# Three banks for attention's logits, four rectified buffers, and the first modulations gathered group by group

## The chip, the cores and the metric

The kernel runs on one core of a Trainium2 chip. The metric is the device time of one execution in microseconds (us), the median of three runs. Engines are named as in the profile: PE is TensorE, DVE is VectorE, ACT is ScalarE, POOL is GpSimd, SP is SyncE, whose queue issues the transfers. PEld is PE's loading of weights.

## The reference

One inference step of a two-layer encoder, for 1024 prompt tokens and 64 sample tokens (the latter with 256 cached keys and a state). In each layer:

```python
shift, scale, gate = split(silu(c) @ w_ada + b_ada, 3)          # c: one vector for the prompt, one for the sample
h = rms_norm(x, g_pre) * (1 + scale) + shift
q_a, k_a, v_a, gate_a, q_i, k_i, w_i, q_b, k_b, v_b, gate_b = split_cols(h @ w_in)
# rope on q_a, k_a, q_i, k_i, q_b, k_b
score = sum_h relu(q_i[h] . k_i) * w_i[h] * IDX_SCALE           # the indexer, 4 heads
idx = top_k(score within the chunk-causal limit, min(256, S // 4))
o_a = softmax(q_a . k_a[idx] / 8) @ v_a[idx]                    # 8 heads of 64, 2 kv heads
o_b = group_norm(retention(q_b, k_b, v_b, state))               # 4 heads of 128, recurrent
y = rms_norm(concat(o_a * silu(gate_a), o_b * silu(gate_b)) @ w_out, g_post)
x = x + gate * y
```

The outputs are x after both layers, the new rotated keys, values and indexer keys, and the new states, for prompt and sample.

## The kernel before

**Tiles and steps.** x is cut into nine tiles of 128 tokens, eight of the prompt and one of the sample (tile 8). The columns of w_in and w_out are cut into ten chunks for each layer (`KIND`): one for the indexer (324 columns), four retention heads (512 each), the gate (512), two for attention (384) and two for the output (512). A step is one chunk for one tile, so there are 2 x 10 x 9 = 180 steps, chunk by chunk, and within a chunk tile by tile. Every engine's program is written out in the same loop `for i in range(-1, STEPS + 2)`, each step in four quarters `q`; work on step i+1's projection is interleaved with what follows steps i, i-1, i-2. Each engine works strictly in its own order; semaphores join them.

**Projection.** h and w are each split into a high and a low part (`h_hi`, `h_lo`, `w_hi`, `w_lo`), and `project` adds three products (two for the sample tile) into one of two PSUM banks `proj`. ACT makes the high part of a slice of weights (`split_weights`), POOL the low part (`lower_weights`); SP loads raw slices into three buffers (`load_raw`), each behind a wait for the slice three before.

**Before the first projection.** SP issues tables and vectors (`tables_landed`, 13 transfers), x tiles 0 and 1, and then 32 slices of w_ada (`ADA_FIRST`, in the order k outside, group inside) into nine slots of `ada_raw`, eight raw slices of w_in among them. PE transposes the vectors (bank `vec`), ACT makes silu(c), PE multiplies each slice (`ada`, L896) into one of four banks (`ada_banks`: both `proj`, both logit banks), one for each group of 512 columns: groups 0 and 1 are the shift, 2 and 3 the scale, for features 0 to 511 and 512 to 1023. When all is done ACT copies the four banks (L1308), PE turns them to columns (`ada_columns`, L902), DVE adds the bias (`modulate`, L1821) and makes the hidden tile (`take_hidden`, L1770, eight operations in two halves from the banks of `turn_hidden`, L910), ACT rounds it (`split_hidden`, L1138) and POOL makes the low part (`lower_hidden`, L1384). x tiles are squared on ACT (`square_x`, L1120, the squares themselves go to the bank `spare`, only their sum is used), the root is taken on POOL (L1394), and DVE norms x into one of two slots (`norm_input`, L1756). `spare` also takes the products of the later w_ada slices.

**Indexer steps.** DVE ropes the step's rows (`rope`, L1518 to L1535) first. For tiles 2 to 8 PE multiplies queries and keys, by head and by part of up to 512 keys (`dot_keys`, L950), two heads in a quarter, into the two `logit_banks`; ACT rectifies into one of two buffers `relu` (L1258); DVE multiplies by the head's weight and adds into `score` (`weigh_relus`, L1551 and L1554).

**The search.** In the retention and gate steps the 256th score of each query is searched bit by bit, for five tiles (one of them the sample tile) on DVE (`count_pass`, L1580) and for tiles 6 and 7 by sign tests on ACT (`test_bit`, L1287), bit n in the n-th retention step, settled on DVE (`settle_bit`).

**Attention steps.** PE's logits (L950) go to the same two banks; DVE adds the mask and takes the row maximum (`row_maxima`, L1724), which frees the bank; ACT takes the exponential (L1271), PE transposes it, ACT copies it (L1238), PE multiplies by the values (L975).

**Rings.** The banks for logits and for transposes are each a `Ring` of `RB = 2`. The keys of a ring are numbered in PE's order by `plan_units`; `wait_free` waits until the use two before has been taken. `dot_keys` asks for all banks of a quarter before its first matmul:

```python
for h, p in heads:
    logits.wait_free(pe, ("l", g, h, p))
for h, p in heads:
    ...
```

and ACT's rectifying waits for the buffer two before:

```python
if n >= 2:
    act.wait_ge(relu_used, n - 1)
```

## Time and profile before

| | us |
|---|---|
| median of three runs | 1540.69 |
| lowest, highest | 1540.31, 1542.75 |
| the profiled execution | 1545.81 |
| its span, first to last instruction | 1544.0 |
| PE busy in it | 1409.0 |
| DVE busy | 1045.1 |
| ACT busy | 786.5 |
| POOL busy | 411.1 |

The mean granted clock of PE in the profiled execution was 0.981 of full speed. The engines' busy times overlap; a stage's length is set by whichever of them, or whichever chain through several, ends last in it. In windows, the columns are the stretch and its length, then the busy time (and instructions) of PE, PEld, DVE, ACT and POOL, the granted clock, the DMA engines' share and GB/s. In a timeline, square brackets hold the idle time of the engine before the row and what ended it.

### The profile page before, as it was taken

Reading aid. Unit: us, or ns where it says so; the run is one execution under the profiler, and the core shown is the slowest. Engines: PE = TensorE matmul, PEld = TensorE weight load, DVE = VectorE, ACT = ScalarE, POOL = GpSimd, SP = SyncE. Lnnn points to the kernel's source line nnn. Section 1 sums busy time; section 2 is a strip of 40 time slices with the busy share of each in tenths; the row PEclk is TensorE's granted clock in tenths of the full one; section 3 lists DMA queues with packets and bytes.
Section 4 is the critical chain, followed back from the end, with each engine's and each line's share of the span. In section 5 each row is a group of like instructions: output and inputs, shape, how many; then the busy total and the mean of one; then the engine's idle time right before and its main releaser. Section 6 shows DMA issues by size and latency. Waiting matters only on the chain.

```text
span 1544.0 us, 24320 instructions
## 1 busy us (share of the span) xinstructions
PE 1409.0 (91%) x7591; PEld 1063.4 (69%) x7591; DVE 1045.1 (68%) x3018; ACT 786.5 (51%) x1916; POOL 411.1 (27%) x360
## 2 busy tenths in 40 slices
PE   6778999999999889889996899999999988988995
PEld 1654777777887567557875567878888756755884
DVE  0687899999996446542287789999998644654224
ACT  2445666666226456554453566666622655555421
POOL 2441233433421001001188114444442101100100
PEclk9899999999999999999998999999999999999998
DMA  9321343423232112112252111211122211211324
GB/s 325 98 69 30 111 130 101 125 89 104 54 86 60 39 31 67 54 56 96 83 184 68 32 44 34 63 45 36 55 66 79 59 32 34 67 59 56 110 69 163
DMA packets 125191, 122.04 MB, mean 79 GB/s; under 512 B 33257, under 2 KB 94025, under 8 KB 125065
## 3 DMA queue, kind: packets, MB, share of 16 engines
q1 hardware_dynamic: 125064, 120.49, 25.8%
q8 instruction: 63, 1.03, 0.3%
q14 instruction: 64, 0.52, 0.1%
HBM read 93.55 MB, written 26.90 MB: 78 GB/s over the span
## 4 chain that ended last, share of the span: by engine, by line
PE 53%; DVE 31%; issue 5%; ACT 5%; DMA 4%; SPq 1%; DVEq 0%; POOL 0%; ACTq 0%
PE proj L931 10%; PE proj L932 10%; PE proj L934 9%; PE turn L910 8%; PE logit L950 6%; DVE U L1580 5%; PE out_bank L975 4%; DVE U L1770 2%; DVE by_cos_sin L1518 2%; DVE by_cos_sin L1520 2%; DVE turned L1535 2%; DVE score L1554 2%; DVE probsT_more L1653 1%; DMA U<-x_dram 1%; ACT probsT_more L1238 1%
## 5 line engine op out<-in xcount | busy, mean ns | idle before, releaser
L931 PE MATMUL proj<-w_hi,h_hi 128*128 128x512 f32 (+2 forms) x1440 | 578.7, 402 | 2.7 <-ACT U L1174 1.4
L932 PE MATMUL proj<-w_lo,h_hi 128*128 128x512 f32 (+2 forms) x1440 | 538.4, 374 | 0.0
L934 PE MATMUL proj<-w_hi,h_lo 128*128 128x512 f32 (+2 forms) x1280 | 480.2, 375 | 0.0
L1378 POOL TENSOR_TENSOR w_lo<-w_raw,w_hi 128x512 fp32r<-128x512 f32 (+2 forms) x160 | 207.5, 1298 | 832.4 <-ACT w_hi L1130 832.3
L931 PEld LDWEIGHTS proj<-w_hi,h_hi 128*128 128x128 f32 x1440 | 274.2, 190 | 62.1 <-issue 23.3
L932 PEld LDWEIGHTS proj<-w_lo,h_hi 128*128 128x128 f32 x1440 | 274.8, 191 | 31.0
L934 PEld LDWEIGHTS proj<-w_hi,h_lo 128*128 128x128 f32 x1280 | 242.8, 190 | 37.0
L1580 DVE TENSOR_SCALAR_CACHE_REDUCE U<-score,cand 128x384 bf16<-128x384 f32 x310 | 222.6, 752 | 2.2
L950 PE MATMUL logit<-keys,queries 64*128 64x512 f32 (+4 forms) x592 | 141.9, 555 | 42.5 <-DVE row_max L1724 22.8
L1238 ACT ACTIVATE probsT_more<-turn 128x512 f32<-128x512 f32 (+3 forms) x156 | 73.4, 491 | 160.2 <-PE turn L910 128.0
L910 PE MATMUL turn<-ident,U 128*128 128x128 f32 x672 | 107.5, 288 | 17.6 <-ACT probsT_more L1238 8.0
L910 PEld LDWEIGHTS turn<-ident,U 128*128 128x128 f32 x672 | 78.9, 146 | 63.5 <-issue 49.8
L1518 DVE TENSOR_TENSOR by_cos_sin<-rows,cos_b 128x256 f32<-128x256 f32 (+1 forms) x126 | 66.0, 524 | 78.3 <-ACT rows L1178 75.2
L1394 POOL TENSOR_TENSOR rstd<-means,minus_half 128x3 f32<-128x3 f32 (+2 forms) x53 | 40.8, 770 | 264.4 <-DVE means L1706 147.2
L950 PEld LDWEIGHTS logit<-keys,queries 64*128 64x128 f32 x592 | 46.8, 189 | 83.0 <-issue 32.7
L1130 ACT ACTIVATE w_hi<-w_raw 128x512 fp32r<-128x512 f32 (+2 forms) x160 | 95.1, 595 | 14.3 <-DMA w_raw<-in_w_in_dram 14.3
L910 PE MATMUL turn<-ident,turned 128*128 128x128 f32 x306 | 57.7, 286 | 37.1 <-DVE turned L1535 29.5
L1724 DVE CUSTOM_DVE_ANT_0 U<-logit,score 128x512 f32<-128x512 f32 (+3 forms) x108 | 61.8, 582 | 34.4 <-PE logit L950 34.2
L1271 ACT ACTIVATE U<-U,neg_max 128x384 f32<-128x384 f32 (+7 forms) x108 | 81.5, 754 | 3.1 <-DVE neg_max L1729 3.1
L910 PEld LDWEIGHTS turn<-ident,turned 128*128 128x128 f32 x306 | 37.3, 143 | 66.4 <-DVE turned L1535 38.3
L1287 ACT ACTIVATE U<-score,cand 128x896 bf16<-128x896 f32 x62 | 64.5, 1040 | 33.8 <-DVE cand L1618 33.7
L975 PE MATMUL out_bank<-probsT_more,U 128*64 128x256 f32 x468 | 75.2, 385 | 0.0
(173 smaller groups left out, 2055.0 us busy)
## 6 DMA issues: line engine op xcount, KB each, us to landing
w_raw<-in_w_in_dram SPq DMA_DIRECT2D x80, 256.0 KB, 3.2
probsT_more<-in_w_ada_dram SPq DMA_DIRECT2D x64, 256.0 KB, 3.9
score<-mixed_dram SPq DMA_DIRECT2D x36, 256.0 KB, 3.0
score<-in_w_ada_dram SPq DMA_DIRECT2D x32, 256.0 KB, 5.3
w_raw<-in_w_out_dram SPq DMA_DIRECT2D x32, 256.0 KB, 3.3
U<-in_x_prompt_dram SPq DMA_DIRECT2D x14, 512.0 KB, 4.0
mixed_dram<-U SPq DMA_DIRECT2D x24, 192.0 KB, 2.1
gates_dram<-U SPq DMA_DIRECT2D x18, 256.0 KB, 2.2
```

The lines of the kernel that those rows point to most:

```text
L910: ins = nc.tensor.transpose(turns.bank(key)[:, n * P:(n + 1) * P], piece, ident[:])
L931: nc.tensor.matmul(out, h_hi[:, k, tile], hi, start=(k == 0), stop=False)
L932: ins = nc.tensor.matmul(out, h_hi[:, k, tile], lo, start=False, stop=(t == SAMPLE and k == KT - 1))
L934: ins = nc.tensor.matmul(out, h_lo[:, k, tile], hi, start=False, stop=(k == KT - 1))
L950: logits.filled(nc.tensor.matmul(logits.bank(key)[:, 0:m], queries[rows_, HILO[g] % 2, h // 2, :], keys[rows_, k0 + a:k0 + a + m], start=T ...
L975: ins = nc.tensor.matmul(out_bank[HD * pair:HD * pair + HD, 0:256], v, probsT[part + pair][:, :, b * P:(b + 1) * P], start=(kb == 0), stop ...
L1130: nc.scalar.activation(w_hi[:, s % WS, 0:w], w_raw[:, n % RAWS, 0:w], ACT.Copy).then_inc(w_hi_ready, 1)
L1238: turns.take(nc.scalar.activation(probsT[2 * (u % 2) + h // 2][:, h % 2, 0:m], turns.bank(key)[:, 0:m], ACT.Copy), key)
L1271: nc.scalar.activation(probs[n % 4][:, 0:w], probs[n % 4][:, 0:w], ACT.Exp, bias=neg_max[:, n % 4:n % 4 + 1], scale=ATT_SCALE, accum_out=r ...
L1378: nc.gpsimd.tensor_tensor(w_lo[:, s % WS, 0:w], w_raw[:, n % RAWS, 0:w], w_hi[:, s % WS, 0:w].bitcast(F32), ALU.subtract).then_inc(w_lo_re ...
L1518: do(nc.vector.tensor_tensor(by_cos[:, 0:w].rearrange("p (h n) -> p h n", n=half), src.rearrange("p (h n) -> p h n", n=half), cs, ALU.mult))
L1580: ins = nc.vector.tensor_scalar(found[:, n % 2, 0:valid_keys(t)], s, cand[:, j:j + 1].bitcast(F32) if b else 0.0, extra(t), ALU.is_ge, ALU ...
```

## The change

1. **Logit rings.** Attention's logits get a ring of their own over three banks: the two logit banks and `spare`. The indexer's and the retention's stay in a ring of two over the same two banks. `Ring` takes its length from its banks. Where one ring's use follows the other's, PE waits until the last units of the other have been taken.
2. **Squares.** Since `spare` is now attention's, the squares in output steps and those of x for layer 1 are written to SBUF, as bf16, into the first slot of `rows`.
3. **Rectified buffers.** `relu` has four buffers instead of two. They reach into space that the sign tests and `ada_row` use, so their first user waits until all rectified logits have been weighed.
4. **Search.** The sign test of bit n on ACT moves from the n-th retention step to the one after it.
5. **The beginning.** The identity, the columns and the eight small vectors are issued on ACT's queue; SP's first transfer is a slice of w_ada. The slices come group by group, in the order 0, 2, 1, 3; x0 is issued behind slice 7, x1 behind slice 15, raw slices of w_in from slice 9 on; the rotary tables and the causal mask come after the last slice. Each group is copied on ACT when its eight slices are done and turned to columns among the slices of the next groups. The first half of tile 0 (features 0 to 511) needs groups 0 and 2 only; DVE, ACT and POOL make it before groups 1 and 3 are complete. Tile 1's transposes on PE move into the first step's second quarter.

```diff
-ADA_FIRST = [(0, grp, k) for k in range(KT) for grp in range(4)]
+FIRST_GROUPS = (0, 2, 1, 3)
+ADA_FIRST = [(0, grp, k) for grp in FIRST_GROUPS for k in range(KT)]
...
+ATT_LOGITS = [key for key in LOGITS if key[0] == "l" and kind(key[1]) == "att"]
+LOGITS = [key for key in LOGITS if key not in set(ATT_LOGITS)]
...
+RELUS = 4
...
-    n = (lct(g)[1] - RET0) * NT + lct(g)[2]
-    return n if n < BITS else None
+    n = (lct(g)[1] - RET0) * NT + lct(g)[2] - 1
+    return n if 0 <= n < BITS else None
...
+    def place(self, key):
+        return self.at[key] % len(self.banks), self.at[key] // len(self.banks)
...
-        relu = U[:, 4096:5120].rearrange("p (s n) -> p s n", s=2)
+        square_dump = rows[:, 0, :].bitcast(BF16)[:, 0:512]
+        relu = [U[:, 4096:4608], U[:, 4608:5120], U[:, 5120:5632], probs_last[:, 0:512]]
...
+        att_logits = Ring([*logit_banks, spare], ATT_LOGIT_AT, att_full, att_taken)
...
         @block.sync
         def _(sp):
-            for dst, src in ((cos_b, t_cos_b), (sin_b, t_sin_b),
-                             (ident, t_ident), (causal, t_causal), (cols, t_cols)):
-                sp.dma_start(dst[:], src).then_inc(tables_landed, 16)
...
-            load_input(0)
-            load_input(1)
...
                 sp.dma_start(ada_raw[:, a % ADAS, :], w_ada[l, k * P:(k + 1) * P, grp * 512:(grp + 1) * 512])\
                   .then_inc(ada_landed[a % ADAS], 16)
-                if a >= 5 and a % 2 and raw < KT:
+                if a in (7, 15):
+                    load_input(a // 8)
+                if a >= 9 and a % 2 and raw < KT:
                     load_raw(raw)
                     raw += 1
+            for dst, src in ((cos_b, t_cos_b), (sin_b, t_sin_b), (causal, t_causal)):
+                sp.dma_start(dst[:], src).then_inc(tables_landed, 16)
...
+                if heads[0] == (0, 0) and lct(g)[1:] == (ATT0, 0):
+                    for key in [k for k in LOGITS if k[1] < g][-RB:]:
+                        logits.wait_taken(pe, key)
+                    pe.wait_ge(ada_copied, len(ADA_GROUPS))
+                if heads[0] == (0, 0) and lct(g)[1:] == (0, SEARCHED[0]) and lct(g)[0]:
+                    for key in [k for k in ATT_LOGITS if k[1] < g][-3:]:
+                        att_logits.wait_taken(pe, key)
...
-            for a, (l, grp, k) in enumerate(ADA_FIRST):
-                pe.wait_ge(ada_landed[a % ADAS], 16 * (a // ADAS + 1))
-                ada(ada_banks[grp], grp, k, ada_raw[:, a % ADAS, :])
-            for grp in range(4):
-                pe.wait_ge(ada_rows_ready, grp + 1)
-                ins = ada_columns(out_bank[:, 8 * grp:8 * grp + 8], ada_rows[grp])
-            ins.then_inc(ada_used, 1)
...
-            turn_hidden(0, 0)
-            turn_hidden(0, 1)
+            def turn_group(n):
+                grp = FIRST_GROUPS[n]
+                pe.wait_ge(ada_rows_ready, n + 1)
+                ada_columns(out_bank[:, 8 * grp:8 * grp + 8], ada_rows[grp]).then_inc(ada_turned, 1)
+
+            for a, (l, grp, k) in enumerate(ADA_FIRST):
+                pe.wait_ge(ada_landed[a % ADAS], 16 * (a // ADAS + 1))
+                ada(ada_banks[grp], grp, k, ada_raw[:, a % ADAS, :])
+                if a % KT == 3 and a > KT:
+                    turn_group(a // KT - 1)
+                if a == 3 * KT - 1:
+                    turn_hidden(0, 0)
+            turn_group(3)
+            pe.wait_ge(ada_turned, 4)
...
+                    if i == -1 and q == 1:
+                        turn_hidden(0, 1)
...
         @block.scalar
         def _(act):
+            for dst, src in ((ident, t_ident), (cols, t_cols)):
+                act.dma_start(dst[:], src).then_inc(rows_landed, 16)
...
-                nc.scalar.activation(spare[:], src, ACT.Square, scale=D ** -0.5, accum_out=total).then_inc(signal, 1)
+                nc.scalar.activation(dump, src, ACT.Square, scale=D ** -0.5, accum_out=total).then_inc(signal, 1)
...
-                        if n >= 2:
-                            act.wait_ge(relu_used, n - 1)
+                        if n >= RELUS:
+                            act.wait_ge(relu_used, n - RELUS + 1)
...
-            for t in (0, 1):
-                wait_x(act, t)
-                square_x(t)
-            for s in range(KT):
-                split_weights(s)
-            for grp in range(4):
-                act.wait_ge(ada_used, len(ADA_FIRST) - 4 + grp + 1)
-                nc.scalar.activation(ada_rows[grp], ada_banks[grp][:], ACT.Copy).then_inc(ada_rows_ready, 1)
+            copy_group(0)
+            wait_x(act, 0)
+            square_x(0)
+            for s in range(4):
                 split_weights(s)
+            copy_group(1)
+            wait_x(act, 1)
+            square_x(1)
+            for s in range(4, KT):
+                split_weights(s)
+            split_half(0)
+            copy_group(2)
+            copy_group(3)
+            split_half(1)
             for t in (2, 3):
                 wait_x(act, t)
                 square_x(t)
-            split_hidden(0, 0)
...
+            modulate_half(0)
+            take_hidden(0, 0, (0,))
+            modulate_half(1)
+            take_hidden(0, 0, (1,))
             norm_input(2, mean_squares(2 + XLAG, 1, 2))
             take_hidden(0, 1)
+            dve.wait_ge(tables_landed, 16 * 3)
```

`copy_group(n)` copies group `FIRST_GROUPS[n]` once its eight slices are multiplied, `split_half(u)` is one half of the former `split_hidden(0, 0)`, and `modulate_half(u)` adds the bias and the pre-gain for half the features, behind the columns of two groups.

## Rows read from the trace of the kernel before

**Rows 1.** The page, busy time and share of each engine

```profile
PE 1409.0 (91%) x7591; PEld 1063.4 (69%) x7591; DVE 1045.1 (68%) x3018; ACT 786.5 (51%) x1916; POOL 411.1 (27%) x360
```

**Rows 2.** Windows by stage: indexer, retention, attention of layer 0; indexer of layer 1

```profile
47.70:149.40 101.70, 77.21 (x402) 55.86 (x403) 76.50 (x167) 48.10 (x115) 40.52 (x32) 0.92 0.24 67
149.40:408.20 258.80, 257.07 (x1371) 200.43 (x1370) 233.81 (x792) 154.35 (x356) 92.52 (x87) 1.00 0.34 101
456.50:688.50 232.00, 209.72 (x1274) 146.04 (x1273) 125.02 (x396) 125.14 (x341) 23.56 (x17) 0.98 0.18 50
812.00:898.50 86.50, 67.41 (x354) 48.17 (x355) 65.56 (x136) 39.91 (x97) 38.06 (x27) 0.94 0.21 51
```

**Rows 3.** Windows of the beginning; last three columns PEclk, DMA share, GB/s

```profile
2.00:4.00 2.00, 0.00 (x0) 0.00 (x0) 0.00 (x0) 0.39 (x1) 0.00 (x0) 1.00 1.03 358
5.00:6.00 1.00, 0.00 (x0) 0.00 (x0) 0.00 (x0) 0.00 (x0) 0.00 (x0) 1.00 0.09 22
12.80:20.00 7.20, 7.11 (x18) 1.46 (x18) 0.75 (x1) 0.95 (x2) 1.96 (x3) 1.00 1.05 378
32.00:38.80 6.80, 6.80 (x22) 1.28 (x19) 0.00 (x0) 1.79 (x3) 0.00 (x0) 1.00 1.05 398
```

**Rows 4.** Timeline of the beginning: start, us, engine, line, operation

```profile
0.72 0.39 SPq L684 DMA_DIRECT2D cos_b<-in_t_dram  x1
...
6.71 2.87 SPq L747 DMA_DIRECT2D score<-in_w_ada_dram  x6
...
6.89 0.42 PE L1033 MATMUL turn<-ident,U 96*128 96x96 f32 x1 [6.89 <-DMA U<-in_g_post_dram]
...
12.79 2.04 PE L896 MATMUL proj<-score,probs_last 128*32 128x512 f32 x3 [5.48 <-DMA score<-in_w_ada_dram]
...
38.87 0.60 ACT L1308 ACTIVATE probs_last<-logit 128x512 f32<-128x512 f32 x1
...
41.46 1.03 PE L902 MATMUL out_bank<-cols,probs_last 128*128 128x2 f32 x8
...
43.10 2.64 DVE L1770 TENSOR_SCALAR U<-turn,pre_scale,pre_shift 128x128 f32<-128x128 f32 x8
...
49.00 0.75 DVE L1756 TENSOR_SCALAR U<-U,rstd 128x1024 f32<-128x1024 f32 x1 [3.19 <-POOL h_lo L1384]
```

**Rows 5.** Timeline, later slices of w_ada on PE

```profile
152.21 1.06 PE L896 MATMUL spare<-probsT_more,probs_last 128*32 128x512 f32 x8
```

**Rows 6.** Groups by line, 92 to 150 us; last: idle before, what ended it

```profile
L1554 DVE SCALAR_TENSOR_TENSOR score<-U,w_idx,score 128x512 f32<-128x512 f32 (+3 forms) x27 | 19.6, 724 | 12.0 <-ACT U L1258 10.0
```

**Rows 7.** The same, 845 to 899 us

```profile
L1554 DVE SCALAR_TENSOR_TENSOR score<-U,w_idx,score 128x512 f32<-128x512 f32 (+3 forms) x30 | 19.7, 658 | 9.9 <-ACT U L1258 7.1 <-DVE score L1554 0.5
```

**Rows 8.** Windows of the last two indexer steps of layer 0

```profile
129.12:139.21 10.09, 9.01 (x43) 4.96 (x42) 7.06 (x16) 5.66 (x14) 0.00 (x0) 1.00 0.13 31
139.21:150.00 10.79, 9.67 (x41) 5.22 (x41) 7.53 (x13) 5.78 (x14) 1.47 (x1) 1.00 0.20 51
```

**Rows 9.** Waits of PE: in total, times, longest

```profile
PE logit L950 <- DVE row_max L1724: 22.8, 16, 2.9
```

**Rows 10.** Timeline of an attention step

```profile
548.42 0.68 DVE L1724 CUSTOM_DVE_ANT_0 U<-logit,score 128x512 f32<-128x512 f32 x1
...
549.03 0.68 DVE L1724 CUSTOM_DVE_ANT_0 U<-logit,score 128x512 f32<-128x512 f32 x1
...
549.87 2.08 PE L950 MATMUL logit<-keys,queries 64*128 64x512 f32 x4 [2.94 <-DVE row_max L1724]
```

**Rows 11.** Groups by line: a square into PSUM, a copy into SBUF

```profile
L1120 ACT ACTIVATE spare<-proj 128x512 f32<-128x512 f32 x36 | 21.4, 594 | 0.0
...
L1189 ACT ACTIVATE score<-proj 128x512 f32<-128x512 f32 x18 | 10.7, 595 | 42.4 <-PE proj L934 40.9 <-DVE proj L1790 1.5
```

**Rows 12.** Timeline of ACT in the first retention step of layer 0

```profile
150.42 0.97 ACT L1287 ACTIVATE U<-score 128x896 bf16<-128x896 f32 x1
...
152.39 0.78 ACT L1258 ACTIVATE U<-logit 128x320 f32<-128x320 f32 x2
```

More of the change, by code:

```diff
@@ L373, in __init__ @@
         self.banks, self.at, self.full, self.taken = banks, at, full, taken
+    def place(self, key):
+        return self.at[key] % len(self.banks), self.at[key] // len(self.banks)
     def bank(self, key):
[L376 removed]
+        return self.banks[self.place(key)[0]]
     def wait_free(self, eng, key):
[L379 to L381 removed]
+        slot, turn = self.place(key)
+        if turn:
+            eng.wait_ge(self.taken[slot], turn)
     def wait_full(self, eng, key):
[L384 to L385 removed]
+        slot, turn = self.place(key)
+        eng.wait_ge(self.full[slot], turn + 1)
     def wait_taken(self, eng, key):
[L388 to L389 removed]
+        slot, turn = self.place(key)
+        eng.wait_ge(self.taken[slot], turn + 1)
     def filled(self, ins, key):
[L392 removed]
+        ins.then_inc(self.full[self.place(key)[0]], 1)
     def take(self, ins, key):
[L395 removed]
+        ins.then_inc(self.taken[self.place(key)[0]], 1)
 class Stores:
@@ L572, in build @@
         logit_taken = [sem(f"logit_taken{n}") for n in range(RB)]
+        att_full = [sem(f"att_full{n}") for n in range(3)]
+        att_taken = [sem(f"att_taken{n}") for n in range(3)]
         relu_used = sem("relu_used")
@@ L949, in dot_keys @@
                     key = ("l", g, h, p)
-                    logits.filled(nc.tensor.matmul(logits.bank(key)[:, 0:m], queries[rows_, HILO[g] % 2, h // 2, :],
+                    ring.filled(nc.tensor.matmul(ring.bank(key)[:, 0:m], queries[rows_, HILO[g] % 2, h // 2, :],
                                                    keys[rows_, k0 + a:k0 + a + m], start=True, stop=True), key)
@@ L1189, in take_projection @@
                     nc.scalar.activation(dst, src[:], ACT.Copy)
-                    square(src[:], squares[:, t, 0, half:half + 1], proj_taken, g + 1)
+                    square(src[:], squares[:, t, 0, half:half + 1], proj_taken, g + 1, square_dump)
             def square_x(n):
@@ L1195, in square_x @@
                 for u in (0, 1):
-                    square(xt(n)[:, u * 512:(u + 1) * 512], squares[:, t + XLAG, 1, u:u + 1], x_squared, 2 * n + u + 1)
+                    square(xt(n)[:, u * 512:(u + 1) * 512], squares[:, t + XLAG, 1, u:u + 1], x_squared, 2 * n + u + 1,
+                           spare[:] if n < NT else square_dump)
             def take_turn(g):
@@ L1255, in middle @@
                         logits.wait_full(act, key)
-                        if n >= 2:
-                            act.wait_ge(relu_used, n - 1)
-                        logits.take(nc.scalar.activation(relu[:, n % 2, 0:m], logits.bank(key)[:, 0:m], ACT.Relu), key)
+                        if n >= RELUS:
+                            act.wait_ge(relu_used, n - RELUS + 1)
+                        logits.take(nc.scalar.activation(relu[n % RELUS][:, 0:m], logits.bank(key)[:, 0:m], ACT.Relu), key)
                         relu_count[0] += 1
@@ L1475, in take @@
                 ring.take(ins, key)
-                n = ring.at[key]
-                last[0] = (ring.taken[n % RB], n // RB + 1)
+                slot, turn = ring.place(key)
+                last[0] = (ring.taken[slot], turn + 1)
             def fence():
```

117 lines of the change are left out of this document (68 added, 49 removed).

## The prediction

> **What bounds the kernel now.** I read the page's busy shares first [rows 1]: TensorE (PE) is busy for 91% of the span, VectorE (DVE) for 68%, and no other engine for more than 51%. Busy shares are means over stages, so the second view is the windows, one for each stage [rows 2]. The reader is to compare PE's busy time with the length of each stretch. In layer 0's retention steps PE is busy 257.07 of 258.80 us: nothing but less PE work helps there, and the change takes no PE work away. In its indexer steps PE is busy 77.21 of 101.70 us at a mean granted clock of 0.92, DVE 76.50; layer 1's are much alike, 67.41 and 65.56 of 86.50. In the attention steps PE is busy 209.72 of 232.00. So waits can be taken out in three places: before the first projection, in the indexer steps, in the attention steps. Whatever they save is kept, since the stages follow each other in every engine's order and nothing waits for a clock time.
>
> The third view is the timeline and the windows of the first 50 us [rows 3, 4]; the fourth the groups by line in the indexer steps [rows 6, 7]; the fifth PE's own waits [rows 9]; and last one attention step in the timeline [rows 10].
>
> **The beginning.** SP issues 13 small tables and vectors from 0.72 us on and two rows of x, and the first slice of w_ada only at 6.71 [rows 4]. The DMA engines were full from 2 to 4 us (share 1.03, the 0.8 MB of rotary tables) and almost idle at 5 to 6 us (0.09); from 12.8 on they run at 1.05 and 378 GB/s, at the end at 398 [rows 3]. That PE is not the limit shows in a later row: eight such matmul instructions, four slices, take 1.06 us when their data are there [rows 5], 0.27 us for a slice, while 256 KB at 388 GB/s take 0.68. So this stretch is the DMA stream, and its tail is serial: the last group's copy starts on ScalarE (ACT) at 38.87, its columns on PE end at 42.49, DVE makes the hidden tile from 43.10 to 45.74, and only when GpSimd (POOL) has lowered it (xn has two slots) DVE norms tile 2, at 49.00 after 3.19 us of waiting [rows 4]. From there DVE has hardly a pause until the retention steps.
>
> After the change SP's first issue is a slice of w_ada. The stream has to bring 32 slices of 256 KB (8.39 MB), x0 and x1 (1.05), eight raw slices of 162 KB (1.33) and 0.15 of vectors and identity: 10.9 MB, or 28.1 us at 388 GB/s (the mean of the two windows). Full from about 2.2 us (as in [rows 3], 2 to 4 us), it ends at 30.3. The three tables (0.83 MB) come behind it; the first rope is their first reader, and now it is behind several more microseconds of work.
>
> What can make the stream run dry: SP may issue nine slices and x0, 2.9 MB, which last until about 9.7 us; then it waits for PE to free a slot. PE needs the vectors, now issued on ACT's queue: ten issues of some 0.4 us from 0.7 on (an issue of a table costs 0.39 [rows 4]), last one at about 4.3. Before they were all landed at 6.89. I take the same 7 us, so PE starts on slices at 7.8 and releases nine at 0.27 us each. SP then issues behind the wait; its raw slices 3 to 7 wait for POOL to lower slice n-3, and on ACT those splits now stand behind the copies of groups 0 and 1 and the squares of x0 and x1. Each such hold-up is 1 to 2 us, and mostly covered by up to nine slices in flight. I add 1.2 us for it: the last slice is used at 31.5, 7.3 us earlier than now.
>
> The tail: copy of the last group 0.7, its columns 1.03, the small modulation ops 0.61 (42.49 to 43.10), then half a tile, four of the eight ops of 2.64 us, 1.32: DVE is through at 35.2 against 45.74 now [rows 4]. The other half was made in the stream's shade: its groups 0 and 2 come first, and split and lowering run on ACT and POOL, which have no other work there. Next, ACT splits the second half (0.6) and squares x2 (two passes of 0.6 us [rows 11] and the reading of each sum, 1.6), the root costs about 1 us on DVE and POOL, and the norm of tile 2 starts at 38.4 against 49.00. **Term: 10.6 us.** Lower bound: if the stream's holes cost 5 us instead of 1.2, 6.8. Upper: 12, if there is none and PE's earlier projection of tile 0 also spares DVE its pause before tile 2.
>
> At this place a rule of the Trainium skill speaks against part of it. "DMA: Bandwidth & Descriptors", section "Issuing engines are not separate DMA queues", says that the queues share 16 engines and that issuing from several saves only sequencer time, usually small beside the transfer. The trace agrees with the first half (share 1.05, nothing to gain in rate) and contradicts the "usually small" here: engines idle at share 0.09 while SP issues. By the rule, with issue time worth nothing, the beginning would gain what rival 2 gains.
>
> **Four rectified buffers.** Now ACT may write rectified logits only two ahead of DVE. At the start of an indexer step DVE does the rope first, so the buffers stay full, ACT stands, the two banks stay full, PE stands, and when DVE comes to weigh heads 2 and 3 they are not there. DVE waited for a rectified logit 10.0 us in layer 0's steps and 7.1 in layer 1's [rows 6, 7]. With four buffers both pairs of a step are rectified before DVE starts to weigh; PE then fills the banks for the next pair while DVE weighs, and DVE should hardly wait. Bounds: 17.1 us if DVE is the limit everywhere. It isn't in the last indexer step of each layer: PE is busy 9.67 of 10.79 us there, because the first projection of the next stage is already 512 wide, against 9.01 of 10.09 (partly stretched by waits) one step before [rows 8]. That caps it. I take off 2 us for each layer: **term 13 us**, range 7 (the step becomes PE-bound through the logits' banks, of which there remain two) to 17.
>
> **Three banks for attention's logits.** PE waited 22.8 us for a row maximum, 16 times [rows 9]. In the row shown, two maxima start at 548.42 and 549.03 (the second ends at 549.72), and PE's pair of heads, which asks for both banks, starts at 549.87 [rows 10]. With a third bank in the ring the second matmul of a pair needs only the first maximum of the pair before: 0.61 us earlier, the distance of the two. The rest of the wait stays, because the rope still stands ahead of the first maximum on DVE. Sixteen waits with a mean of 1.43 us and a longest of 2.9: 16 x 0.61 = 9.8 if each is long enough; some aren't, I count 13. **Term 7.9 us**; from 4, if what follows (the transposed probabilities' copy on ACT) ends last in half of these steps, to 11, if the lower granted clock behind the long waits disappears (the four instructions at 549.87 take 2.08 us).
>
> **Squares into SBUF.** 54 of ACT's squares no longer go to the spare bank. The row of a square from PSUM into PSUM has 594 ns, a copy of equal width from PSUM into SBUF 595 [rows 11]: 54 x 1 ns, nothing. The Trainium skill, "ScalarE: Activation LUTs", section "Step-by-step: what each stage is for", says that ACT writes PSUM with lower latency than SBUF; it gives no figure. The measured rows show no such difference, and the waits sit in ACT's slack.
>
> **The later search.** The two sign tests of a bit leave the first retention step, where they stand ahead of the sample tile's rectified logits on ACT (tests from 150.42, rectifying from 152.39 [rows 12]), and come to a step that had none. That is 2.0 us on ACT in each layer; this stretch is nearly PE-bound, so I take 0.5 each, **1 us**, bounds 0 and 4. The step that gets the tests has cover for them in ACT's slack; with none it would be 0.
>
> **New waits on PE** at the first attention and the first searched indexer step ask for banks released steps before; nothing. Tile 1's transposes move behind the first two quarters of the projection; they need what DVE has done by then.
>
> **Sum.** 10.6 + 13 + 7.9 + 1 = 32.5 us. The profiled execution took 1545.81 us (span 1544.0), so 1513.3 in its terms; it stands 5.1 above the median of 1540.69, which gives **1508.2 us**.
>
> **Rivals.**
> 1. *Partly absorbed.* The indexer steps turn PE-bound after half the gain (6.5) and the attention steps hand back half (4): 10.6 + 6.5 + 4 = 21 us, 1519.6. For it: PE's 9.67 of 10.79. Against: one step before, PE has slack, and PE's own waits are what inflates its busy time.
> 2. *The stream gains only bytes and tail.* PE starts late, because vectors queue behind big slices, or raw slices hold SP: then only the three tables' bytes (0.83 MB, 2.1 us) and the shorter tail (10.6 - 7.3 = 3.3) are gained, 5.4 instead of 10.6: 27 us in all, 1513.4. It decides if PE's first slice is later than about 9.7 us.
> 3. *More than forecast.* The lower clock in the indexer and attention steps (means 0.92 and 0.98 [rows 2]) goes away with the long waits: another 8 us, 1500.
> 4. *Slower.* The clock goes the other way: many short PE gaps in place of a few long ones, and the granted clock stays at the lower level (1.2 GHz) in attention. A PE-bound microsecond at that level does half a microsecond's work, so to eat 32.5 us it needs 65 us more of it than now, and 100 us of it in the two attention stages would give +17 us, 1558. Against: the change shortens PE's waits and adds none, and the retention steps show 1.00.
> 5. *Nothing.* The ring of three is filled in pairs and relu's are not ahead because ACT stands elsewhere, and the stream restarts slowly: within 3 us. It needs all of these, hence little.
>
> **Numbers.** Forecast 1508.2: 0.50. Rival 1: 0.20. Rival 2: 0.13. Rival 3: 0.11. Rival 4: 0.03. Rival 5 with what I have missed: 0.03. The terms' own bounds give 18 to 44 us off; the range that leaves out no more than two in ten is 1498 to 1525. A measurement of this kernel tells a change of 0.2%, 3 us, from none. Faster 0.94, the same 0.03, slower 0.03.
>
> **What would show it.** Right: first slice matmul at about 8 us and the last copy of a modulation group at about 32; the norm of tile 2 at 38; DVE's idle time ahead of the weighing ops near 3 us instead of 17; PE's wait for row maxima at 15 us instead of 22.8, in as many places; the retention stages unchanged in length. Wrong: a gap in the DMA share between 8 and 30 us; PE's idle time in the indexer steps now before the transposes or before ACT's copies; an attention step of equal length with another releaser; a granted clock under 0.9 in a stage that had 1.00. The likeliest single error is the indexer term, where I could not see how much of PE's busy time is work.

## The result, and the profile after

The changed kernel took 1517.14 us in the median of four runs (1513.14 to 1518.44), the kernel before 1540.58 (1540.31 to 1542.75). The ratio is 0.984 with a 95% interval of 0.982 to 0.9861: faster, by 23.4 us between the medians. The forecast was 1508.2, with a range of 1498 to 1525. Timed twice more on other occasions, the changed kernel had 0.9848 (0.9827 to 0.9869) and 0.9825 (0.9807 to 0.9843).

The profiled execution took 1513.14 us (span 1511.3), 32.7 less than the profiled execution before. That this is all but the predicted 32.5 is luck: it is the fastest of its four runs, and the one before stood 5.1 above its median. The times of the runs decide, the traces say in which stage.

The page, busy times [rows 1]:

```profile
PE 1398.7 (93%) x7591; PEld 1058.8 (70%) x7591; DVE 1046.3 (69%) x3021; ACT 784.6 (52%) x1916; POOL 410.7 (27%) x360
```

Windows of the stages of [rows 2] (indexer, retention and attention of layer 0, indexer of layer 1), with the boundaries moved to where the stages now lie:

```profile
42.00:137.70 95.70, 75.57 (x395) 54.83 (x394) 77.04 (x168) 50.56 (x125) 41.17 (x33) 0.93 0.24 72
137.70:396.40 258.70, 256.97 (x1370) 200.31 (x1369) 233.38 (x792) 154.54 (x355) 92.78 (x87) 1.00 0.33 101
444.60:669.70 225.10, 206.89 (x1274) 143.96 (x1273) 124.97 (x396) 125.20 (x341) 23.54 (x17) 0.99 0.18 52
790.00:876.00 86.00, 70.15 (x377) 49.93 (x376) 68.91 (x142) 42.20 (x101) 40.19 (x28) 0.94 0.20 51
```

The retention stretch of layer 0 has kept its length, 258.70 against 258.80 us, and PE fills it as before. PE executes the same 7591 instructions, and is busy 206.89 us in attention where it was 209.72. What went is idle time and, in attention, time at the lower clock (the means of the three other windows are 0.93, 0.99 and 0.94 against 0.92, 0.98 and 0.94).

Stage lengths are read more sharply from ACT's copies of the projection, which come once in a step. The first copy of the indexer and of the retention, layer 0, in the kernel before and then after:

```profile
53.40 0.42 ACT L1160 ACTIVATE rows<-proj 128x324 f32<-128x324 f32 x1
...
149.53 0.51 ACT L1168 ACTIVATE rows<-proj 128x384 f32<-128x384 f32 x1
```

```profile
48.68 0.42 ACT L1196 ACTIVATE rows<-proj 128x324 f32<-128x324 f32 x1
...
137.67 0.51 ACT L1204 ACTIVATE rows<-proj 128x384 f32<-128x384 f32 x1
```

96.13 us in the one, 88.99 in the other. The table has such differences of the first copies of two stages, in us, of this profile and of those of the experiments below:

| from copy to copy | before | after | after_again | begin_only | rest_only | relu2 | att2 |
|---|---|---|---|---|---|---|---|
| start of the first | 53.40 | 48.68 | 49.72 | 48.98 | 52.95 | 49.47 | 48.53 |
| indexer, layer 0 | 96.13 | 88.99 | 90.66 | 98.12 | 87.72 | 97.79 | 89.80 |
| attention, layer 0 | 232.02 | 225.11 | 224.87 | 232.48 | 225.39 | 224.86 | 232.41 |
| indexer, layer 1 | 86.35 | 81.73 | 82.84 | 86.46 | 82.20 | 87.51 | 81.76 |
| attention, layer 1 | 230.53 | 224.85 | 224.83 | 230.87 | 225.10 | 225.07 | 229.63 |
| output, layer 1 | 114.29 | 113.87 | 113.85 | 114.28 | 113.87 | 113.87 | 113.89 |

So in this profile the beginning gave 4.7 us by the first copy, the indexer steps 7.1 and 4.6, the attention steps 6.9 and 5.7. The forecast had 10.6, 13 and 7.9.

The beginning in the timeline, rows that answer to [rows 4]:

```profile
4.34 0.32 ACTq L1136 DMA_DIRECT2D U<-in_g_post_dram  x1
...
5.04 6.77 SPq L749 DMA_DIRECT2D score<-in_w_ada_dram  x2
...
8.71 0.42 PE L1047 MATMUL turn<-ident,U 96*128 96x96 f32 x1 [8.71 <-DMA U<-in_g_post_dram]
...
9.55 3.64 PE L902 MATMUL proj<-score,probs_last 128*32 128x512 f32 x16 [0.41 <-ACT vec L1145]
...
37.82 0.60 ACT L1343 ACTIVATE probs_last<-logit 128x512 f32<-128x512 f32 x1 [3.31 <-PE logit L902]
...
44.28 0.75 DVE L1814 TENSOR_SCALAR U<-U,rstd 128x1024 f32<-128x1024 f32 x1 [0.66 <-POOL rstd L1451]
```

Windows of it, as in [rows 3], and SP's waits in the first 34 us (in total, times, longest):

```profile
10.00:11.00 1.00, 1.00 (x8) 0.20 (x4) 0.00 (x0) 0.00 (x0) 0.00 (x0) 1.00 0.39 150
11.00:12.00 1.00, 1.00 (x8) 0.20 (x4) 0.00 (x0) 0.00 (x0) 0.00 (x0) 1.00 0.01 2
12.00:13.00 1.00, 1.00 (x9) 0.20 (x2) 0.00 (x0) 0.00 (x0) 0.00 (x0) 1.00 0.47 129
13.00:19.00 6.00, 4.99 (x18) 1.26 (x13) 1.51 (x2) 2.76 (x7) 1.42 (x3) 1.00 0.92 281
```

```profile
SPq L749 <- PE proj L902: 7.5, 5, 6.0
SPq L721 <- POOL w_lo L1435: 5.0, 5, 2.1
```

To be seen: the last vector is issued at 4.34 us and PE is released by the vectors at 8.71, not at 7. By then SP has issued nine slices and x0 and stands 6.0 us in its tenth. The DMA engines then run dry: they have a share of 0.39, 0.01 and 0.47 in the three microseconds after 10, and 281 GB/s until 19. The last group's copy starts at 37.82, 1.05 us before that of the kernel before [rows 4]. Behind it everything went as worked out: the norm of tile 2 is 6.5 us behind the copy (predicted 6.9), where it was 10.1.

The waits for rectified logits in layer 0's and layer 1's indexer steps, groups by line, to be read against [rows 6] and [rows 7], and PE's waits for row maxima against [rows 9]:

```profile
L1612 DVE SCALAR_TENSOR_TENSOR score<-U,w_idx,score 128x512 f32<-128x512 f32 (+3 forms) x20 | 17.2, 863 | 4.4 <-ACT U L1295 3.1
```

```profile
L1612 DVE SCALAR_TENSOR_TENSOR score<-U,w_idx,score 128x512 f32<-128x512 f32 (+3 forms) x20 | 13.9, 698 | 4.4 <-ACT U L1295 3.1
```

```profile
PE logit L964 <- DVE row_max L1782: 9.4, 8, 2.3
...
PE spare L964 <- DVE row_max L1782: 5.0, 4, 2.3
```

DVE waited 3.1 us in each layer instead of 10.0 and 7.1 (4.7 in layer 0 in after_again). PE waited 9.4 + 5.0 = 14.4 us for row maxima instead of 22.8, in 12 places instead of 16.

### The profile page after: what moved, and what is told of

The parts are those of the page before. It is cut to its first block, busy times and chain, and to the rows that moved or that the text cites. A ratio compares the mean times of both kernels' runs of the same rounds, so it can differ in the third digit from the quotient of the medians.

```text
span 1511.3 us, 24328 instructions
## 1 busy us (share of the span) xinstructions
PE 1398.7 (93%) x7591; PEld 1058.8 (70%) x7591; DVE 1046.3 (69%) x3021; ACT 784.6 (52%) x1916; POOL 410.7 (27%) x360
## 4 chain that ended last, share of the span: by engine, by line
PE 56%; DVE 28%; issue 5%; ACT 5%; DMA 4%; POOL 0%; SPq 0%; DVEq 0%; ACTq 0%; POOLq 0%
PE proj L937 11%; PE proj L938 11%; PE proj L940 10%; PE turn L916 8%; DVE U L1638 5%; PE logit L964 5%; PE out_bank L989 5%; DVE U L1828 2%; DVE by_cos_sin L1576 2%; PE spare L964 2%; DVE by_cos_sin L1578 2%; DMA U<-x_dram 1%; DVE turned L1593 1%; DVE probsT_more L1711 1%; ACT probsT_more L1275 1%
## 5 line engine op out<-in xcount | busy, mean ns | idle before, releaser
L1325 ACT ACTIVATE probsT_more<-score,cand 128x1024 bf16<-128x1024 f32 x62 | 70.4, 1135 | 0.0
```

Source lines behind the costliest of these rows:

```text
L1325: nc.scalar.activation(tested[n % 2][:, 0:valid_keys(t)], scores(t)[:, 0:valid_keys(t)], ACT.Sign, bias=cand[:, col:col + 1].bitcast(F32) ...
```

## The experiments

There were eleven runs, of nine kernels (the changed kernel and rest_only ran twice), in three groups; each group was timed beside the kernel before on the same chip (medians 1542.91, 1541.97 and 1543.66 us). A ratio below is to these; 0.001 of it is 1.5 us. A label stands for a run and for its kernel.

**1 and 2. The change cut in two.** begin_only is the kernel before with part 5 of the change alone, rest_only the changed kernel without it:

```diff
 # begin_only
+FIRST_GROUPS = (0, 2, 1, 3)
+ADA_FIRST = [(0, grp, k) for grp in FIRST_GROUPS for k in range(KT)]
...
 # rest_only
-FIRST_GROUPS = (0, 2, 1, 3)
-ADA_FIRST = [(0, grp, k) for grp in FIRST_GROUPS for k in range(KT)]
+ADA_FIRST = [(0, grp, k) for k in range(KT) for grp in range(4)]
```

(with all that belongs to the beginning: the queues, copy_group, turn_group, the halves of tile 0).

> The kernel before with the change's beginning alone (issues on ACT's queue, slices group by group, half a tile early). Theory from the two traces: the stream ran dry from 10 to 13 us, so the beginning brings 4.7 us, 1535.9 against 1540.6. The forecast's term was 10.6: 1530.0; if the other parts of the change disturb the beginning, it should show here.

> Everything but the beginning. Theory: what the changed kernel has left, 23.4 - 4.7 = 18.7 us, so 1521.9. Rival: the parts are not additive, since another beginning moves where the lower granted clock falls in later stages; then begin_only and rest_only together bring more or less than 23.4 by 3 us or more.

begin_only: 1540.72 us, ratio 0.9986 (0.9974 to 0.9998), 2.2 us. rest_only: 1518.14, 0.9843 (0.982 to 0.9865), 24.2 us. The beginning fell far short of 10.6, and of the 4.7 that the first two profiles had let expect; its interval is 0.3 to 4.0 us. The rest brought a little more than its 21.9, and 5 us more than the 18.7 expected of it. Together they are 26.4 us, where the three timings of the changed kernel gave 24.6, 23.4 and 27.0: whether the two halves add up can't be told from these. In begin_only's timeline PE is released by the vectors at 9.93:

```profile
9.93 0.42 PE L1024 MATMUL turn<-ident,U 96*128 96x96 f32 x1 [9.93 <-DMA U<-in_g_post_dram]
```

By the first copy begin_only is 4.4 us ahead of the kernel before, but its indexer steps then take 98.12 us instead of 96.13: they had a granted clock of 0.50 in the first step and 0.82 from 100 us on, where the kernel before had 0.88 and 0.89:

```profile
49.00:59.10 10.10, 7.72 (x28) 7.27 (x29) 6.86 (x12) 3.85 (x11) 7.97 (x7) 0.50 0.27 76
...
100.00:147.00 47.00, 39.39 (x163) 23.87 (x164) 32.07 (x63) 20.14 (x50) 6.80 (x6) 0.82 0.11 26
```

```profile
53.40:63.60 10.20, 5.90 (x33) 5.35 (x31) 7.49 (x15) 3.98 (x11) 8.08 (x7) 0.88 0.26 76
...
103.00:149.50 46.50, 36.67 (x163) 21.63 (x164) 32.83 (x64) 20.88 (x51) 7.47 (x7) 0.89 0.11 26
```

**3 and 4. One ring shortened at a time.** The changed kernel with two rectified buffers, and with two banks for attention:

```diff
 # relu2
-RELUS = 4
+RELUS = 2
 # att2
-        att_logits = Ring([*logit_banks, spare], ATT_LOGIT_AT, att_full, att_taken)
+        att_logits = Ring(logit_banks, ATT_LOGIT_AT, att_full, att_taken)
...
-                    for key in [k for k in ATT_LOGITS if k[1] < g][-3:]:
+                    for key in [k for k in ATT_LOGITS if k[1] < g][-2:]:
```

> The changed kernel with two rectified buffers instead of four. Theory: the indexer steps and the first retention step lose again what the traces gave them (7.1 + 4.6 us, 11.7), 1528.8. Rival: PE's bound and the two remaining logit banks give half of it in any case, 1523. The attention stages must not change in length.

> The changed kernel with attention's ring cut to the two logit banks. Theory: 8.4 us of PE's waits for row maxima come back, 1525.5, with 22 to 23 us of waits as before. Rival: the trace's 12.6 us of shorter attention stages are all the third bank's, clock included, and 1529.7 comes out. The indexer steps must not change.

relu2: 1528.01 us, 0.9908 (0.9885 to 0.9932). att2: 1527.87, 0.9908 (0.9886 to 0.993). Against the changed kernel's three ratios (0.984, 0.9848, 0.9825) each part is worth 0.0060 to 0.0083, 9 to 13 us; the expectations were 11.7 for the buffers and 8.4 or 12.6 for the bank. The stage table puts them in their places: without the four buffers the indexer steps take 97.79 and 87.51 us, 11.8 more in sum than in after_again and 14.6 more than in the first profile; without the third bank attention takes 232.41 and 229.63, 12.3 more than in after_again. Each undoing leaves the other's stages alone. The groups of relu2 in layer 0's indexer steps and the waits of att2 show the mechanisms come back whole:

```profile
L1612 DVE SCALAR_TENSOR_TENSOR score<-U,w_idx,score 128x512 f32<-128x512 f32 (+3 forms) x30 | 23.0, 767 | 14.0 <-ACT U L1295 11.6
```

```profile
PE logit L964 <- DVE row_max L1782: 22.8, 16, 2.9
```

11.6 us of waiting for rectified logits again, and the same 22.8 in 16 places as [rows 9].

**5 to 7. The vectors' queue.** The changed kernel again; the six vectors of bias and gains issued on SP ahead of the slices (identity, columns and the two conditions stay on ACT); and all ten small transfers on SP:

```diff
 # split_vectors (sp_vectors: the identity, the columns and the conditions as well)
         def _(sp):
+            r = 2 * KT
+            for l in range(DEPTH):
+                for src in (b_ada, g_pre, g_post):
+                    n = src.shape[1] // P
+                    sp.dma_start(vec_rows[r:r + n, :], ...).then_inc(rows_landed, 16)
+                    r += n
...
         def _(act):
-            for l in range(DEPTH):
-                for src in (b_ada, g_pre, g_post):
-                    n = src.shape[1] // P
-                    act.dma_start(vec_rows[r:r + n, :], ...).then_inc(rows_landed, 16)
-                    r += n
```

> The changed kernel once more, beside the same runs of the kernel before as the next three. Before's runs spread over 9 us (1538.7 to 1547.7), so a single profiled execution of either may stand some 5 us off its median. Expected 1517 to 1520; a span 3 us or more above the first profile's 1511.3 would come from the steps of the indexer stage, where a GpSimd operation that starts just before VectorE's ropes may cost 2 us (1.22 and 1.56 us instead of 0.23 and 0.48).

> The changed kernel with six of the small vectors issued on SP ahead of the slices, four transfers left on ACT's queue. Theory: the vectors landed late (8.7 us, 4.3 after their last issue) because they were issued behind slices on full engines; so PE freed no slot until 11 us and the engines stood idle from 10 to 13 us. Then here the vectors land by about 5, the stream starts 2 us later but never stops, and the last copy of a group comes 3 us earlier, 34.8 instead of 37.8: 1514.5. Rival: the stream's rate, not the hole, is the limit (229 to 313 GB/s after it, with raw slices among them), and it ends at 37 to 38 as before.

> All ten small transfers on SP ahead of the slices, none on ACT's queue; otherwise the changed kernel. Theory: the first slice is issued only at about 4.5 us, two later than with the split, the vectors land at 6: the last copy at 36 to 36.5, 1516. If issue time is what counts and contention nothing, it is worse than the changed kernel by 3.8 us, copy at 41, 1521.

after_again: 1519.44 us, 0.9848 (0.9827 to 0.9869); vectors at 9.92, last copy at 38.86. split_vectors: 1513.02, 0.981 (0.979 to 0.983). sp_vectors: 1517.04, 0.9834 (0.9815 to 0.9853); vectors at 5.52, last copy at 38.26. split_vectors in the timeline, the window that had the hole and the next, and SP's waits:

```profile
4.19 0.42 PE L1054 MATMUL turn<-ident,U 96*128 96x96 f32 x1 [4.19 <-DMA U<-in_g_post_dram]
6.02 6.59 PE L909 MATMUL proj<-score,probs_last 128*32 128x512 f32 x16 [1.40 <-DMA score<-in_w_ada_dram]
```

```profile
10.00:13.00 3.00, 2.61 (x9) 0.50 (x6) 0.00 (x0) 0.35 (x1) 0.00 (x0) 1.00 0.98 343
13.00:19.00 6.00, 5.11 (x20) 1.66 (x20) 1.51 (x2) 2.99 (x8) 2.27 (x3) 1.00 1.06 397
```

```profile
SPq L728 <- POOL w_lo L1436: 6.1, 5, 2.0
SPq L756 <- PE proj L909: 2.6, 7, 0.5
```

With the vectors there at 4.19 the hole is gone (share 0.98, then 1.06), and SP's longest wait for PE is 0.5 us. The last group's copy starts at 36.50 and the norm of tile 2 at 42.97, 2.4 us before those of after_again, its neighbour in the runs. The time is 6.4 us less there by the medians, though against the changed kernel's other ratios (0.984 and 0.9825) only 5 and 2 us. The edit changes two things at once: the last vector is issued at 2.57 instead of 4.34 us, and it lands 1.6 us behind its issue instead of 4.4. sp_vectors closes the hole too, but its stream starts later by ten issues, and gains little: 2.4 us by the medians, where the intervals overlap. Its last copy is only 0.6 us before that of after_again. All last copies came later than expected of these kernels (36.50 for 34.8, 38.26 for 36 to 36.5).

**8. What holds SP next.** In split_vectors SP stands 6.1 us for lowered slices. This kernel lets ACT split slices 4 and 5 of w_in before it squares x1, and POOL lower them before that root:

```diff
 # split_x1_later = split_vectors and
             copy_group(1)
+            for s in (4, 5):
+                split_weights(s)
             wait_x(act, 1)
             square_x(1)
-            for s in range(4, KT):
+            for s in (6, 7):
                 split_weights(s)
```

> split_vectors, and ACT squares x1 after the split of raw slices 4 and 5, not before it (GpSimd's root likewise), so that SP is held less by raw slices 6 and 7. Theory: in the changed kernel SP waited 5.0 us for lowered slices, and its last eight slices were issued only from 27.9 us: another 1 us, last copy at 33.5. Rival: enough slices are in flight and nothing changes against split_vectors.

1512.88 us, 0.9811 (0.9792 to 0.983). The trace shows the edit at work: 387 GB/s from 26 to 34 us, where split_vectors had 332, the last copy at 35.16 (33.5 was expected) and the norm of tile 2 at 41.64, another 1.3 us earlier:

```profile
26.00:34.00 8.00, 7.72 (x41) 3.36 (x43) 3.85 (x9) 2.87 (x7) 3.98 (x5) 1.00 1.06 387
```

The time is that of split_vectors within 0.1 us. A gain of 1.3 us could not be told from none in four or five runs; the two are the fastest of all kernels here.

**9 to 11. Does the beginning's gain last?** rest_only and the changed kernel had been timed in different groups and stood 1.3 us apart; in the traces rest_only caught up within one step. So both were timed side by side, with the split vectors on the kernel before (the edit of split_vectors on begin_only):

> The same kernel as rest_only, timed beside the changed kernel on one chip, since the two had been timed in different calls and stood within 1.3 us. Theory A (the beginning's gain is real and adds to the rest): 2 to 4 us slower than the changed kernel, ratio near 0.9850. Theory B (what the beginning gains at the first projection is lost in the indexer steps behind it, where the first step takes 10.2 us in the changed kernel and took 7.4 in this one): within 1.5 us of the changed kernel, and the first step again at about 7.4 us.

> The changed kernel itself. Theory A: ratio 0.983, 2 to 4 us below rest_five. Theory B: ratio 0.9845, the same as rest_five within 1.5 us; first copy of an indexer step at 48.5 to 50 us against 53, the step behind it 10.2 us long at a granted clock near 0.5, against 7.4 us at about 0.93.

> The kernel before with the change's beginning alone, and the six vectors of bias and gains issued on SP ahead of the slices. If the late vectors are what the beginning lost, it is 5 to 8 us faster than the kernel before (ratio 0.995 to 0.9965), where the beginning as changed was 2.2 us faster (0.9986), with the vectors landed near 4.2 us and the last group's copy at 36.5. If the indexer steps behind give back whatever the beginning gains, it stays at 0.998 or above.

rest_five: 1519.69 us, 0.9848 (0.983 to 0.9866). after_five: 1515.83, 0.9825 (0.9807 to 0.9843): 3.9 us less by the medians. begin_split: 1538.43, 0.9969 (0.9958 to 0.998), 4.8 us, a little less than the 5 to 8 expected, against 2.2 for begin_only. This speaks for the first theory: the beginning adds to the rest, by 2 to 4 us, and more with the vectors in time. It is no proof: the intervals of rest_five and after_five overlap, and in the groups before rest_only's ratio (0.9843) lay between two of the changed kernel's (0.984 and 0.9848).

Part of the gain at the first copy is handed back all the same. In every profile with the new beginning, layer 0's indexer steps are longer than in those without it and with as many buffers: 97.79 (relu2), 98.12 (begin_only) and 97.78 us (begin_split) against 96.13 with two, 88.99 to 90.66 in seven profiles against 87.72 (rest_only) and 88.86 (rest_five) with four. begin_split is 5.8 us ahead at the first copy and 4.4 at the last one of the kernel. One difference between these traces is where PE was at the lower clock. The kernel before had 6.8 us of it ahead of the first copy and 13.7 in the indexer steps of layer 0, begin_only none and 34.1; rest_five had 10.2 and 13.7, after_five none and 17.1. That this is the cause is not shown.

What did belong to one execution is the short first step. The first indexer step of rest_only and of rest_five, one and the same program:

```profile
52.95 0.44 ACT L1185 ACTIVATE rows<-proj 128x324 f32<-128x324 f32 x1 [0.82 <-PE proj L949]
...
60.33 0.44 ACT L1185 ACTIVATE rows<-proj 128x324 f32<-128x324 f32 x1 [0.75 <-PE proj L949]
```

```profile
53.51 0.42 ACT L1185 ACTIVATE rows<-proj 128x324 f32<-128x324 f32 x1
...
63.51 0.44 ACT L1185 ACTIVATE rows<-proj 128x324 f32<-128x324 f32 x1 [1.07 <-PE proj L949]
```

7.38 us in one and 10.00 in the other. In rest_only DVE's two rotations began before POOL's operation did, the second by 0.13 us; in rest_five, as in the profile of the kernel before and the three of the changed one, POOL began first and they took longer. Of the 2.62 us between the two first steps 1.1 are left at the end of the stage (87.72 against 88.86). Timelines of DVE and POOL in rest_only, then in rest_five:

```profile
57.76 0.23 DVE L1562 TENSOR_TENSOR turned<-by_cos_sin 128x64 f32<-128x64 f32 x1
57.90 0.48 DVE L1564 TENSOR_TENSOR turned<-by_cos_sin 128x320 f32<-128x320 f32 x1
58.03 1.49 POOL L1413 TENSOR_TENSOR h_lo<-U,h_hi 128x512 fp32r<-128x512 f32 x1
```

```profile
58.32 2.48 POOL L1413 TENSOR_TENSOR h_lo<-U,h_hi 128x512 fp32r<-128x512 f32 x2
58.46 1.20 DVE L1562 TENSOR_TENSOR turned<-by_cos_sin 128x64 f32<-128x64 f32 x1
59.58 1.57 DVE L1564 TENSOR_TENSOR turned<-by_cos_sin 128x320 f32<-128x320 f32 x1
```

## Why the prediction was right and wrong

**The beginning is the step that failed.** It was put at 10.6 us and measured 2.2 alone and 3.9 on top of the rest, with 3.7 to 4.9 at the first copy in the six profiles that have it as changed, set against that of the kernel before. Its tail was right (6.5 us from the last copy to the norm of tile 2, predicted 6.9). The stream was not: the last copy came at 37.82, and at 38.86 and 38.49 in the later profiles, instead of 31.5. Three sentences of the prediction carried it.

- "I take the same 7 us". The vectors landed at 8.71, 9.92 and 8.98 us. The 7 us came from a trace in which they had the DMA engines almost to themselves [rows 3]; after the change their last issue, at 4.34, lies among slices on full engines, and landed 4.4 us later in the first profile. With six of them ahead of the slices, and issued earlier (split_vectors), the hole at 10 to 13 us goes.
- "releases nine at 0.27 us each". The price was that of a later row [rows 5]. Here eight slices (sixteen instructions) take 3.64 us, 0.46 each, and SP stands 6.0 us in its tenth slice, to about 11.4, that is 1.8 us after PE began.
- "Whatever they save is kept". begin_only was 4.4 us ahead at the first copy and 2.2 by its timing; the indexer steps of layer 0 hand some of the start back, as shown above.

The last term of the stream, "I add 1.2 us" for SP's waits behind POOL, was about right. These waits are 5.0 us in all, but nearly all of them lie between 17 and 27.6 us, and from 19 to 26 the engines moved 391 GB/s in spite of them: the slices in flight cover most. From 26 to 34 us split_vectors has 332 GB/s, and split_x1_later, with 387 there, gets 1.3 us back.

In bytes: by 30 us the changed kernel had moved 299 GB/s x 30 us = 9.0 MB, where the working had 10.9 MB in at 30.3. The missing 1.9 MB are 5.0 us at 388 GB/s, of the 6.3 by which the last copy was late; 1.5 MB of them, 3.9 us, are missing from 10 to 19 us, in the hole and the slow restart behind it (219 GB/s). split_x1_later had 9.7 MB by then (324 GB/s), its last copy still 3.7 us behind the forecast: 3.1 of them are the missing 1.2 MB, more than half of it from 2 to 4 us, where its slices come behind six issues and it moved 53 GB/s.

**Rival 2 is what happened there**, at 0.13: it had 5.4 us for the beginning, and its mark, a first slice on PE later than about 9.7 us, was crossed in two of three profiles (10.75 and 9.82) and missed by 0.15 in the first (9.55). Its mechanism, vectors that queue behind big slices, is the one that split_vectors shows. The prediction had named the sign to look for, a gap in the DMA share between 8 and 30 us.

**Four rectified buffers** were right: 13 us predicted; 11.8 to 14.6 by stage lengths against relu2, 9 to 13 by the times. The limit that was named, PE in the last indexer step, is there: PE is busy 10.35 of the last 10.70 us of layer 0's indexer steps. So rival 1's half gain is excluded. DVE's idle time fell to 6.2 us, not to 3, without harm to the sum.

**Three banks** were right in mechanism and too small in size: 7.9 us predicted, 12.1 to 12.3 by stage lengths, 9 to 13 by the times. The waits gave 8.4 of them, near what was worked out, though in 12 places and not in as many as before. The row of [rows 10], where PE stood 2.94 us before its pair of heads, now reads

```profile
534.25 2.08 PE L964 MATMUL logit<-keys,queries 64*128 64x512 f32 x4 [2.33 <-DVE row_max L1782]
```

that is 0.61 us less, the distance of two maxima. Most of the rest is the granted clock. In the windows below, before and then after, PE was at the lower level for (1 - mean) x length / 0.5: 3.4, 6.9 and 6.8 us before, 3.4 and 3.4 after, and these are all such stretches of the two attention stages. Ten microseconds less of it are up to 5 us of PE work. att2 tells the two apart: in layer 1 it too had 3.4 us at the lower level, and is 4.8 us longer than the changed kernel (229.63 against 224.85), of which 4.3 are waits for row maxima (11.4 against 7.1); and with 3.4 us less at that level than the kernel before it is 0.9 us shorter (229.63 against 230.53). By that the 10.3 us are worth about 3, an estimate; with the 8.4 of the waits that leaves 1 to 2 of the 12.6 us by which the two stages became shorter, and these stay open.

```profile
514.50:519.50 5.00, 4.33 (x16) 2.91 (x16) 1.83 (x8) 1.68 (x4) 0.00 (x0) 0.66 0.27 51
548.60:556.40 7.80, 6.40 (x21) 4.16 (x23) 3.88 (x13) 2.25 (x5) 0.00 (x0) 0.56 0.03 6
1275.00:1284.00 9.00, 7.00 (x23) 4.29 (x23) 4.48 (x15) 2.84 (x6) 0.01 (x1) 0.62 0.07 19
```

```profile
533.50:538.00 4.50, 3.61 (x11) 1.89 (x11) 2.70 (x8) 0.73 (x4) 0.00 (x0) 0.62 0.04 7
1250.00:1255.00 5.00, 4.86 (x22) 3.36 (x19) 2.76 (x9) 2.22 (x4) 0.00 (x0) 0.66 0.10 29
```

This is part of rival 3, which had been given 8 us over both kinds of steps; the indexer steps show next to none of it (means 0.93 and 0.94).

**The later search** was put at 1 us, half of it in each layer; it brought nothing in layer 0 and 1.2 us in layer 1. The first retention step of layer 0, from copy to copy, takes 8.03 to 8.05 us in all thirteen profiles. That of layer 1 takes 6.54 to 6.56 us in the three kernels without this part (before, begin_only, begin_split) and 5.36 to 5.39 in the ten profiles with it. relu2 and att2 are among the ten, so neither the buffers nor the third bank make it; the squares moved in the same ten, and only the timeline tells them from this part. The timeline of PE in that step, before and then after, shows the mechanism that the prediction named: ACT's two tests stood ahead of the sample tile's rectified logits, and PE, with its next pair of heads, waited 1.10 us for these. After the change it doesn't.

```profile
903.74 0.81 PE L950 MATMUL logit<-keys,queries 64*128 64x320 f32 x4 [1.10 <-ACT U L1258]
```

```profile
878.46 0.81 PE L964 MATMUL logit<-keys,queries 64*128 64x320 f32 x4
```

**The squares** were put at nothing. Layer 1's output steps took 113.85 to 113.93 us with them in SBUF, and 114.29, 114.28 and 113.95 (begin_split) with them in PSUM: 0.4 us at most, and not settled by three traces. A square of a projection takes 591 ns where it took 594, and the reading of its sum 204 where it took 188. The 18 squares of x for layer 1, which read SBUF, take 630 ns into SBUF where they took 602 into PSUM. The page "ScalarE: Activation LUTs" of the Trainium skill, section "Step-by-step: what each stage is for", has PSUM as the quicker target. The squares of x agree, by 29 ns, though what is written also became bf16; those of the projection do not. The rows of the prediction could not show the former: they had a copy for the one target and a square for the other.

**The sum.** Without the beginning 21.9 us were predicted and 24.2 and 23.5 measured. With the beginning at 2 to 4 instead of 10.6 that makes 26 to 28, and the three timings of the changed kernel gave 24.6, 23.4 and 27.0 by their ratios. So of the 8.9 us by which the forecast missed 7 to 8 are the beginning's; the rest brought back 2; and 2 to 4 stay, as much as the timings of one kernel differ among themselves. They are not put down to any step.

## What to carry to other kernels

When small transfers move from a quiet time to the start of a big stream, their landing time is no longer that of the old trace: price them by what the queue ahead of them holds, and look who waits for them, here PE and through it SP. Nine slots in flight did not bridge one late vector. A ring's length can be priced well from the trace, as the distance between the release that is asked for and the one that will do, times the waits that are long enough. A microsecond gained at the start is not yet one gained at the end. And a part that moves a start by a few microseconds is proved by runs side by side, not by two profiles, since a step's length can hang on which of two engines comes first by 0.1 us.

## What the runs showed of the hardware

- A rotation on DVE that began after POOL had begun to make the low part of the hidden tile took 1.20 us instead of 0.23 (64 columns) and 1.57 instead of 0.48 (320 columns). In rest_only the second one began 0.13 us before POOL's operation, ran beside it and took 0.48. So some 0.1 us decide, and these two operations are 2.06 of the 2.62 us between the two first steps.
- The ten small transfers of 0.13 MB in all had their last issue at 4.34 us and landed at 8.71; in split_vectors, with six on SP and four on ACT at the same time, the last issue at 2.57 and no slice ahead of them, the last landed at 4.19.
- PE's first slices took 1.06 us an instruction at a recorded clock of 1.00, four instructions starting together every 0.86 us; later ones took 0.59 to 0.62. Groups of the line from 9 to 14 us, and over the whole beginning:

```profile
L902 PE MATMUL proj<-score,probs_last x16: 1061/1061/1061, 9.5 to 12.1; 128*32 128x512 f32 x16
```

```profile
L902 PE MATMUL logit<-score,probs_last x24: 592/617/1061, 13.0 to 34.6; 128*32 128x512 f32 x24
```
